# The first experts on tokens sorted by group into tiles of 128, with the token tiles stationary and the weights moving

## The chip, the cores and the metric

The kernel is one program on one core of a Trainium2 chip. It holds its state in on-chip memory and streams every large weight from HBM once. The metric is the device time of one execution in microseconds (us), lower being better. PE is the matmul engine, DVE the vector engine, ACT the scalar engine, POOL the third elementwise engine, SP the engine that issues the weight transfers.

## The reference

Two blocks run one after the other, all in float32. The first has 256 tokens (272 with the meta tokens) of width 1024: a mixer, an output projection `w_out`, and then, on the normalised rows, a two-level mixture of 16 experts of hidden width 256, in 4 groups of 4:

```python
g_sel = argmax(x @ w_rg + b_rg)                    # one group of 4 for each token
p_g = softmax(group logits)[g_sel]
e_prob = softmax(expert logits of that group)      # 4 experts
top_p, top_i = top_k(e_prob, 2); top_p /= sum(top_p)
combine[token, expert] = p_g * top_p               # zero for 14 of 16 experts
for e in range(16):
    h = silu(x @ w_gate[e]) * (x @ w_up[e])        # 1024 -> 256
    y = y + combine[:, e:e+1] * (h @ w_down[e])    # 256 -> 1024
```

The second block has two layers on 512 tokens (256 of them a context): two gated feed-forward parts each, attention between them, all modulated by a vector that is itself a product with a large matrix, `w_ada`. The result must agree to float32 accuracy.

## The kernel before

**Weights in units.** Every weight is streamed as a *unit* of 1 MB (128 partitions of 2048 elements) into one of two `raw` buffers, by SP. ACT writes its high part `w_hi` (L601), DVE its low part `w_lo`, which is `raw` minus `w_hi` (L1046). The rows of the tokens are split likewise (`u_hi`, `u_lo`), and PE forms each product as three matmuls, high by high, high by low and low by high (L1864, L1865, L1866 in `products`). A 128x128 block of weights is stationary, and the tokens move, 256 columns in the first block's experts and 512 in the second block.

**The experts.** All 256 tokens go through all 16 experts. In `moe_a` (32 units, 48 matmuls of 256 columns each) PE makes gate and up; ACT takes silu, DVE multiplies by the share `comb` of the token (L1564) and by the other product (L1567), ACT makes the high part of the hidden rows and POOL the low part (`hm_lo`, L1785). In `moe_b` (16 units of 48 such matmuls) all the hidden rows are multiplied by `w_down`, which adds into the rows `h`. The routing (logits L2320 on PE, then some 40 small operations of 128x8 on DVE) stands after the first expert unit's split and runs beside the first units.

**Beside them.** Each quarter chunk of the modulation vector (1 MB of `w_ada`) is loaded by ACT and summed into `ada_acc` by four operations of 128x512 on DVE (L1067; L1064 for the first two of a chunk). PE sums each of the four chunks over partitions with 16 matmuls of one column (L2048). POOL squares the context rows for a mean (L1808 to L1811); DVE's reciprocal of it is L1603. During `moe_b` DVE and ACT also make the normalised context rows (`l0a`) of the second block. Then comes `f1a`, the second block's first feed-forward, whose unit 0 runs first on 256 rows at a time.

**Order.** Each engine runs its program in the order written, with semaphores between engines; loops `linear`, `ffn_up` and `ffn_down` go over units, and what stands beside a unit is called from them by its number. SP loads a unit when the low and high parts of the one that had its buffer are done.

## Time and profile before

| | |
|---|---|
| three runs | 2247.23, 2250.8 and 2251.64 us, median 2250.8 |
| the profiled execution | span 2245.4 us from first to last instruction; its own time beside the span is not given |
| busy share of the span | PE 97%, DVE 61%, ACT 34%, POOL 23% |
| chain that ended last | PE 85% of it, DVE 8%, ACT 3%, DMA 2% |
| first expert matmul | 150.80 us |
| end of the experts, first matmul of f1a | 443.37 us |
| first 512-column matmul of f1a unit 1 | 457.06 us |
| DMA in the whole span | 314.68 MB, mean 140 GB/s |

The profile is of one execution. A time is from the start of the span. "Busy" does not count waiting, but an instruction that is held up once started is counted as busy for as long as it takes. A duration in a group is the mean, and matmuls overlap, so their rate is read from starts that follow one another.

### The profile page before, as it was taken

The numbers are of one execution on the slowest core, as the hardware profiler recorded it, in microseconds if no ns is written. First come the engines' busy times: TensorE is split into PE (matmuls) and PEld (weight loads), VectorE is DVE, ScalarE is ACT, GpSimd is POOL, SyncE is SP. The second block draws the span as 40 slices with busy tenths as digits, with TensorE's granted clock in tenths as the row PEclk, the third lists the DMA queues.
The fourth block names the chain that finished last, engine by engine and source line by source line (L and its number), as shares of the span: only waits on it lengthen the run. The fifth ranks groups of instructions, "written<-read, shape, count | busy, mean of one in ns | idle before, by whom it ended". The sixth has DMA issues, their size and how long they took to land.

```text
span 2245.4 us, 31895 instructions
## 1 busy us (share of the span) xinstructions
PE 2185.8 (97%) x13297; PEld 1905.4 (85%) x13297; DVE 1368.7 (61%) x1770; ACT 764.9 (34%) x1075; POOL 517.5 (23%) x243
## 2 busy tenths in 40 slices
PE   7989999999999999999999999999999999899998
PEld 7889999988888888757988888898888888679998
DVE  6567875577775247796677772246655226765443
ACT  4344444432222232374322222242222223454443
POOL 0014542122221100153122221112222110243431
PEclk9999999999999999999999999999999999999999
DMA  5347876656664336301366653346663336205664
GB/s 163 106 103 213 220 224 182 176 169 175 177 173 115 92 104 180 95 20 57 110 175 185 183 155 91 97 113 187 187 187 110 96 97 168 80 1 144 179 170 147
DMA packets 474005, 314.68 MB, mean 140 GB/s; under 512 B 27503, under 2 KB 435958, under 8 KB 473862
## 3 DMA queue, kind: packets, MB, share of 16 engines
q1 hardware_dynamic: 434304, 237.02, 37.8%
q10 hardware_dynamic: 39558, 75.64, 10.8%
q8 instruction: 105, 1.72, 0.3%
q14 instruction: 38, 0.31, 0.0%
HBM read 311.56 MB, written 1.05 MB: 139 GB/s over the span
## 4 chain that ended last, share of the span: by engine, by line
PE 85%; DVE 8%; ACT 3%; DMA 2%; issue 1%; SPq 1%; POOL 0%; DVEq 0%; ACTq 0%
PE ps L1864 26%; PE ps L1866 25%; PE ps L1865 25%; DVE w_lo L1046 3%; PE ps L2048 2%; ACT w_hi L601 2%; PE ps L1857 2%; PE ps L2491 1%; PE ps L2453 1%; DVE st L1703 1%; DMA raw<-in_w_ffn_down 1%; DVE u_lo L1139 1%; DMA raw<-in_w_in 1%; SPq L572 1%; DVE tmp_a L1131 1%
## 5 line engine op out<-in xcount | busy, mean ns | idle before, releaser
L1864 PE MATMUL ps<-u_hi,w_hi 128*128 128x256 f32 (+2 forms) x2624 | 887.3, 338 | 16.5 <-DVE u_lo L1139 6.2
L1866 PE MATMUL ps<-u_hi,w_lo 128*128 128x256 f32 (+2 forms) x2624 | 875.6, 334 | 0.0
L1865 PE MATMUL ps<-u_lo,w_hi 128*128 128x256 f32 (+2 forms) x2624 | 875.2, 334 | 0.0
L1046 DVE TENSOR_TENSOR w_lo<-raw,w_hi 128x2048 fp32r<-128x2048 f32 (+1 forms) x238 | 504.4, 2119 | 341.2 <-ACT w_hi L601 340.9
L601 ACT CAST w_hi<-raw 128x2048 fp32r<-128x2048 f32 (+1 forms) x238 | 418.4, 1758 | 468.7 <-PE ps L1866 411.9
L1864 PEld LDWEIGHTS ps<-u_hi,w_hi 128*128 128x128 f32 x2624 | 500.4, 191 | 69.8 <-DVE w_lo L1046 9.7
L1866 PEld LDWEIGHTS ps<-u_hi,w_lo 128*128 128x128 f32 x2624 | 500.2, 191 | 49.0
L1865 PEld LDWEIGHTS ps<-u_lo,w_hi 128*128 128x128 f32 x2624 | 500.7, 191 | 46.9
L1785 POOL TENSOR_TENSOR hf_lo<-tmp_b,hf_hi 128x512 fp32r<-128x512 f32 (+1 forms) x88 | 240.6, 2734 | 713.2 <-ACT hf_hi L744 713.2
L1067 DVE SCALAR_TENSOR_TENSOR ada_acc<-ada_w,sc_c,ada_acc 128x512 f32<-128x512 f32 x448 | 348.3, 834 | 7.8 <-DMA ada_w<-in_w_ada 2.0
L1864 PE MATMUL ps<-hf_hi,w_hi 128*128 128x512 f32 (+1 forms) x770 | 270.6, 351 | 1.0 <-DVE w_lo L1046 0.8
L1865 PE MATMUL ps<-hf_lo,w_hi 128*128 128x512 f32 (+1 forms) x770 | 269.3, 350 | 0.0
L1866 PE MATMUL ps<-hf_hi,w_lo 128*128 128x512 f32 (+1 forms) x770 | 269.3, 350 | 0.0
L741 ACT ACTIVATE tmp_a<-ps 128x512 f32<-128x512 f32 (+1 forms) x88 | 47.9, 545 | 614.1 <-PE ps L1866 449.7
L1198 DVE TENSOR_TENSOR tmp_b<-tmp_a,ps 128x512 f32<-128x512 f32 (+1 forms) x88 | 54.6, 621 | 185.5 <-ACT tmp_a L741 185.5
L1864 PEld LDWEIGHTS ps<-hf_hi,w_hi 128*128 128x128 f32 x770 | 144.9, 188 | 22.4 <-DVE w_lo L1046 1.0
L1866 PEld LDWEIGHTS ps<-hf_hi,w_lo 128*128 128x128 f32 x770 | 144.9, 188 | 21.1
L1865 PEld LDWEIGHTS ps<-hf_lo,w_hi 128*128 128x128 f32 x770 | 144.8, 188 | 21.1
L1800 POOL TENSOR_TENSOR sq_sum<-sq_sum,tmp_b 128x512 f32<-128x512 f32 (+1 forms) x37 | 75.4, 2038 | 297.8 <-ACT tmp_b L627 250.4
L1845 POOL TENSOR_SCALAR s<-s,st 128x512 f32<-128x512 f32 (+1 forms) x48 | 78.9, 1648 | 143.7 <-DVE st L1718 143.7
L1785 POOL TENSOR_TENSOR hm_lo<-tmp_b,hm_hi 128x256 fp32r<-128x256 f32 x32 | 75.3, 2353 | 123.5 <-ACT hm_hi L864 123.5
L1256 DVE SCALAR_TENSOR_TENSOR h<-ps,gate,h 128x256 f32<-128x256 f32 x50 | 22.3, 480 | 105.7 <-PE ps L1866 105.7
(314 smaller groups left out, 1903.9 us busy)
## 6 DMA issues: line engine op xcount, KB each, us to landing
ada_w<-in_w_ada ACTq DMA_DIRECT2D x144, 512.0 KB, 4.0
raw<-in_w_ffn_gate SPq DMA_DIRECT2D x88, 512.0 KB, 4.0
raw<-in_w_ffn_up SPq DMA_DIRECT2D x88, 512.0 KB, 5.3
raw<-in_w_in SPq DMA_DIRECT2D x52, 512.0 KB, 5.0
...
```

Of the source, the lines that this page charges most:

```text
L601: nc.scalar.copy(w_hi[:, slot, 0:elems], raw[:, slot, 0:elems]).then_inc(hi_done.sem, 1)
L741: nc.scalar.activation(tmp_a[:, n % 2, 0:T], ps[:, 2 * (g % 2), 0:T], ACT.Silu).then_inc(sig["silu"].sem, 1)
L1046: tt(w_lo[:, slot, 0:elems], raw[:, slot, 0:elems], w_hi[:, slot, 0:elems].bitcast(F32), ALU.subtract).then_inc(lo_done.sem, 1)
L1067: ins = stt(out=ada_acc[:, v, :], in0=ada_w[:, slot, kk, :], scalar=sc_c[:, k, v:v + 1], in1=ada_acc[:, v, :], op0=ALU.mult, op1=ALU.add)
L1198: tt(tmp_b[:, n % 2, 0:T], tmp_a[:, n % 2, 0:T], ps[:, 2 * (g % 2) + 1, 0:T], ALU.mult).then_inc(acc_free.sem, 1)
L1785: tt(lo[:, n, 0:T], tmp_b[:, n % 2, 0:T], hi[:, n, 0:T].bitcast(F32), ALU.subtract).then_inc(sig["lo"].sem, 1)
L1800: tt(sq_sum[:, 0:T], sq_sum[:, 0:T], tmp_b[:, k % 2, 0:T], ALU.add).then_inc(n["summed"].sem, 1)
L1845: ins = nc.gpsimd.tensor_scalar(s[:, x, 1, c0:c1], s[:, x, 1, c0:c1], st[:, i % 4, 0, nq + q:nq + q + 1], None, ALU.mult)
L1857: return nc.tensor.transpose(dst, src, ident[0:n, 0:n])
L1864: mm(acc, w1, m_hi, start=(first and i == 0), stop=False)
L1865: mm(acc, w1, m_lo, start=False, stop=False)
L1866: ins = mm(acc, w2, m_hi, start=False, stop=(last and i == n - 1))
```

## The change

The numbers of lines in this section are those of the changed kernel.

**Sorting.** After the group of each token is known, DVE works out a slot for it (position within its group, by three matmuls against a triangle; a token past the 128th of its group goes to a fifth tile) and builds a 0/1 matrix `place` (two tiles of 128 tokens by 640 slots). PE turns the rows `u_hi` and `u_lo` to tokens by columns (`turn_tokens`, 32 transposes), and `gather` multiplies them by `place` into the tiles: four tiles, one for each group, and a spill tile for the group that has more than 128 tokens. ACT and DVE copy them out as `x_hi` and `x_lo`. The shares of the slots come by 20 small float32 matmuls (`slot_shares`).

**Twenty steps.** A step is one tile through one expert: five tiles of four experts. `up_part` has the tile stationary and the weights moving, 8 blocks by 3 matmuls of 512 columns (256 of gate, 256 of up). ACT takes silu, DVE multiplies by share and up in one operation (`hid`, L1756, 128x256), PE turns `hid` by two transposes during the next step, ACT and DVE split it (`ht_hi`, `ht_lo` L1724), and `down_part` adds 12 matmuls of 512 columns to two banks that hold the tile's output for its four experts. Each four steps, ACT and DVE split a tile's output (`tile_rest`); at the end `scatter` multiplies the tiles by `place` turned, 80 matmuls of 256 columns, back into rows that are added to `h`.

**Units.** There are 60 units of expert weights instead of 48, three for a step, since the spill tile's group is loaded again, its number read by SP from a register. They go through a ring of five raw buffers (two old, three in space not yet used) and three for the parts.

**Low parts.** `vector_cols` divides them: POOL makes the whole low part of the second unit (`M0 + 1`, 128x2048), and half (128x1024) of the unit of `w_down` of each step; DVE makes the rest. In all POOL makes 11 of 60 units' worth. The low part of the hidden rows, which POOL made, is DVE's now.

**Moved.** The context rows' squares go from beside the experts to the time right after the context rows come out of PE (about 52 us), ahead of the mixer's masks on POOL. Their root and reciprocal go from `moe_b` to ahead of the routing. The mean squares of the final norm are made by token, by PE from squares of ACT. The normalised context rows come in the last two steps. A quarter of the modulation vector stands in each of the steps 1 to 16. The load of the last unit of `w_out` comes after a wait for the mixer's sums, behind a table of 400 KB, the router's weights and unit `M0 + 1`.

```diff
+        M0, M1 = st_moe["u0"], st_moe["u0"] + st_moe["units"]
+
+        def gate_unit(i):
+
+            return M0 + max(3 * i - 1, 0)
+
+        def down_unit(i):
+
+            return M0 + min(3 * i + 4, 3 * STEPS - 1)
+
+        downs = {down_unit(i): i for i in range(STEPS)}
+        RAW_RING, W_RING = (2, 3, 4, 0, 1), (0, 1, 2)
+        raw_of = [RAW_RING[(u - M0) % 5] if M0 <= u < M1 else u % 2 for u in range(N_UNITS)]
+        w_of = [W_RING[(u - M0) % 3] if M0 <= u < M1 else u % 2 for u in range(N_UNITS)]
...
+        def vector_cols(u):
+
+            if u >= N_UNITS:
+                return 0
+            return 0 if u == M0 + 1 else 4 if u in downs else KD
...
+            nc.vector.reciprocal(rstd[:, SEQ:T2], rstd[:, SEQ:T2]).then_inc(ev["ctx_rstd"], 1)
...
+            def tile_low(k):
+
+                dve.wait_ge(ev["gathered"], 2 * k + 2)
+                nc.vector.tensor_copy(x_lo[:, k, :], ps[:, GATHER_BANKS[k % 2][1], :]).then_inc(ev["x_low"], 1)
...
+            def hidden_low(i):
+
+                dve.wait_ge(ev["ht_high"], i + 1)
+                tt(ht_lo[:, i % 2, :, :], ps[:, 5, HID * (i % 2):HID * (i % 2) + HID].rearrange("p (k t) -> p k t", k=2),
+                   ht_hi[:, i % 2, :, :].bitcast(F32), ALU.subtract).then_inc(ev["ht_low"], 1)
...
+            for i in range(STEPS):
+                if i:
+                    hidden_low(i - 1)
+                    split_lo(gate_unit(i) + 3)
...
+                dve.wait_ge(ev["m_silu"], i + 1)
+                stt(out=hid[:, i % 2, :], in0=gated_up[:, i % 2, :], scalar=share[:, i // 4, i % 4:i % 4 + 1],
+                    in1=ps[:, i % 2, HID:2 * HID], op0=ALU.mult, op1=ALU.mult).then_inc(ev["m_hid"], 1)
+                work, complete = ada_at("moe", i)
+                if complete is not None:
+                    ada_out(complete)
+                split_lo(gate_unit(i) + (4 if i else 3))
+                split_lo(gate_unit(i) + (5 if i else 4))
...
+                for c, quarter in work:
+                    ada_quarter(c, quarter)
...
+                pool.wait_ge(hi_done.sem, u + 1)
+                n = vector_cols(u)
+                tt(w_view(w_lo, u_lo, u)[:, n:KD, :], raw_view(u)[:, n:KD, :], w_view(w_hi, u_hi, u)[:, n:KD, :].bitcast(F32),
+                   ALU.subtract).then_inc(lo_pool.sem, 1)
...
+            pool.wait_ge(rows_out.sem, rows_out.at(12))
+            context_squares()
...
             square_sums("ffn1", SEQ)
-            pool.wait_ge(rows_out.sem, rows_out.at(12))
-            ffn_up(moe_sig, SEQ, MOE_F, hm_hi, hm_lo, context_squares)
-            square_sums("end1", T2, norm_of["l0a"])
+            split_lo(M0 + 1)
+            for i in range(STEPS):
+                split_lo(down_unit(i))
...
+            def gather(k):
+
+                if k >= 2:
+                    pe.wait_ge(ev["x_high"], k - 1)
+                    pe.wait_ge(ev["x_low"], k - 1)
+                for bank, ut in zip(GATHER_BANKS[k % 2], (ut_hi, ut_lo)):
+                    for t in range(2):
+                        ins = mm(ps[:, bank, :], ut[:, t, P * k:P * k + P], place[:, t, 0:4 * P], start=(t == 0), stop=(t == 1))
+                    ins.then_inc(ev["gathered"], 1)
...
+            def up_part(i, k):
+
+                u = gate_unit(i) + k // 4
+                j = 2 * (k % 4)
+                m_hi, m_lo = [tile_out(i // 4, part)[:, k, :] for part in range(2)]
+                acc = wide(i % 2)
+                high, low = two_eighths(u, w_hi, u_hi, j), two_eighths(u, w_lo, u_lo, j)
+                mm(acc, m_hi, high, start=(k == 0), stop=False)
+                mm(acc, m_lo, high, start=False, stop=False)
+                ins = mm(acc, m_hi, low, start=False, stop=(k == KD - 1))
+                if k % 4 == 3:
+                    ins.then_inc(unit_done.sem, 1)
+
+            def turn_hidden(i):
+
+                pe.wait_ge(ev["m_hid"], i + 1)
+                if i:
+                    pe.wait_ge(ev["ht_low"], i)
+                for k in range(2):
+                    c0 = HID * (i % 2) + P * k
+                    ins = turn(ps[:, 5, c0:c0 + P], hid[:, i % 2, P * k:P * k + P], P)
+                ins.then_inc(ev["hid_turned"], 1)
+
+            def down_part(i):
+
+                u, e = down_unit(i), i % 4
+                begin(u, None)
+                pe.wait_ge(ev["ht_low"], i + 1)
+                if e == 0 and i:
+                    pe.wait_ge(ev["y_low"], i // 2)
+                if i == 0:
+                    pe.wait_ge(ev["x_low"], KD)
+                for half in range(2):
+                    acc = wide(2 + half)
+                    for k in range(2):
...
+            pe.wait_ge(ev["places"], 1)
+            gather(0)
+            gather(1)
+            begin(M0, None)
+            for k in range(KD):
+                if k == 4:
+                    begin(M0 + 1, None)
+                pe.wait_ge(ev["x_high"], k + 1)
+                pe.wait_ge(ev["x_low"], k + 1)
+                up_part(0, k)
+                if k + 2 < KD:
+                    gather(k + 2)
+            slot_shares()
+            for i in range(1, STEPS):
+                begin(gate_unit(i), None)
+                if i >= 2:
+                    pe.wait_ge(ev["m_hid"], i - 1)
+                if i == STEPS - PER_GROUP:
+                    pe.wait_ge(ev["xb_high"], 2)
+                    pe.wait_ge(ev["xb_low"], 2)
+                for k in range(4):
+                    up_part(i, k)
+                    if k == 1:
+                        turn_hidden(i - 1)
+                complete = ada_at("moe", i)[1]
+                if complete is not None:
+                    ada_sums(complete)
+                begin(gate_unit(i) + 1, None)
+                for k in range(4, KD):
+                    up_part(i, k)
+                if i in (2, 3):
+                    gather_spill(i - 2)
+                if 5 <= i < 5 + TILES:
+                    turn_places(i - 5)
+                down_part(i - 1)
+            turn_hidden(STEPS - 1)
+            pe.wait_ge(ev["place_rows"], TILES)
+            scatter(0, 0, TILES - 1)
+            scatter(1, 0, TILES - 1)
+            down_part(STEPS - 1)
```

DVE in the middle of `moe_a` before: one unit after another, `tmp_a` and `tmp_b` being silu times share and the hidden rows.

```order
L1564 TENSOR_TENSOR tmp_a<-tmp_a,comb 128x256
L1567 TENSOR_TENSOR tmp_b<-tmp_a,ps 128x256
L1046 TENSOR_TENSOR w_lo<-raw,w_hi 128x2048
L1067 SCALAR_TENSOR_TENSOR ada_acc<-ada_w,sc_c,ada_acc 128x512 x4
L1564 TENSOR_TENSOR tmp_a<-tmp_a,comb 128x256
L1567 TENSOR_TENSOR tmp_b<-tmp_a,ps 128x256
L1046 TENSOR_TENSOR w_lo<-raw,w_hi 128x2048
```

DVE in the middle of the steps now; the first row is the hidden rows of the step before, and `u_lo` is the third buffer for low parts.

```order
L1724 TENSOR_TENSOR ht_lo<-ps,ht_hi 128x256
L1181 TENSOR_TENSOR u_lo<-h,u_hi 128x8x256
L1756 SCALAR_TENSOR_TENSOR hid<-gated_up,share,ps 128x256
L1181 TENSOR_TENSOR w_lo<-raw_92,w_hi 128x2048
L1181 TENSOR_TENSOR w_lo<-raw_93,w_hi 128x1024
L1200 SCALAR_TENSOR_TENSOR ada_acc<-ada_w,sc_c,ada_acc 128x512 x4
L1724 TENSOR_TENSOR ht_lo<-ps,ht_hi 128x256
```

One step has two and a half low parts, of 5120 elements, one quarter of the vector and two operations of 256, where two units of `moe_a` had two low parts, four operations of 256 and one quarter.

PE at the start of a step now (`x_hi`, `x_lo` the tile's rows, stationary, `u_hi`, `u_lo` the first unit's parts, moving), with the turn of the hidden rows of the step before.

```order
L2590 MATMUL ps<-u_hi,x_lo 128x512
L2591 MATMUL ps<-u_lo,x_hi 128x512
L2589 MATMUL ps<-u_hi,x_hi 128x512
L2590 MATMUL ps<-u_hi,x_lo 128x512
L2591 MATMUL ps<-u_lo,x_hi 128x512
L2035 MATMUL ps<-base,hid 128x128 x2
L2589 MATMUL ps<-u_hi,x_hi 128x512
```

And at its end, where the last block of `up_part` (here from the first buffer for parts) and the end of the one before are followed by the first of `down_part`'s 12.

```order
L2591 MATMUL ps<-w_lo,x_hi 128x512
L2589 MATMUL ps<-w_hi,x_hi 128x512
L2590 MATMUL ps<-w_hi,x_lo 128x512
L2591 MATMUL ps<-w_lo,x_hi 128x512
L2620 MATMUL ps<-w_hi,ht_hi 128x512
L2621 MATMUL ps<-w_hi,ht_lo 128x512
L2622 MATMUL ps<-w_lo,ht_hi 128x512
```

The turn stands after 6 of 24 matmuls, and what it yields must be split by ACT and DVE before `down_part`, which comes 18 matmuls later.

POOL before, from the norm ahead of the router into the experts.

```order
L1800 TENSOR_TENSOR sq_sum<-sq_sum,tmp_b 128x256 x4
L1785 TENSOR_TENSOR hm_lo<-tmp_b,hm_hi 128x256 x9
L1808 TENSOR_TENSOR rstd<-h 128x256
L1785 TENSOR_TENSOR hm_lo<-tmp_b,hm_hi 128x256
L1810 TENSOR_TENSOR tmp_b<-h 128x256
```

POOL now at the same place.

```order
L1994 AFFINE_SELECT sT<-sT 64x256 x4
L1958 TENSOR_TENSOR sq_sum<-tmp_b 128x256
L1961 TENSOR_TENSOR sq_sum<-sq_sum,tmp_b 128x256 x4
L1981 TENSOR_TENSOR w_lo<-raw_92,w_hi 128x2048
L1981 TENSOR_TENSOR w_lo<-raw,w_hi 128x1024
L1981 TENSOR_TENSOR w_lo<-raw_93,w_hi 128x1024
L1981 TENSOR_TENSOR w_lo<-h,w_hi 128x1024
```

The norm's sums are followed at once by the low part of the whole unit `M0 + 1`, and then by a half for each step; between them POOL only waits.

## Rows read from the trace of the kernel before

**Rows 1.** Stretches: length, busy time of each engine, granted clock, DMA share, GB/s.
```profile
40.00:60.00 20.00, 19.63 (x154) 19.34 (x153) 16.09 (x29) 13.42 (x21) 0.00 (x0) 1.00 0.43 139
140.00:150.00 10.00, 7.14 (x37) 4.12 (x37) 6.62 (x19) 6.17 (x13) 0.21 (x1) 0.69 0.38 102
150.80:443.37 292.57, 290.46 (x2409) 287.81 (x2407) 212.75 (x256) 123.92 (x148) 104.11 (x53) 1.00 0.72 198
443.37:457.06 13.69, 13.69 (x114) 13.58 (x113) 9.51 (x20) 8.48 (x14) 0.00 (x0) 1.00 0.29 77
940.00:960.00 20.00, 15.49 (x95) 11.54 (x93) 13.55 (x29) 12.97 (x37) 5.79 (x5) 1.00 0.19 58
```

**Rows 2.** Timeline of PE: start, duration, line, operands, shape, count.
```profile
151.04 0.28 PE L1866 MATMUL ps<-u_hi,w_lo 128*128 128x256 f32 x1
151.16 0.28 PE L1864 MATMUL ps<-u_hi,w_hi 128*128 128x256 f32 x1
...
462.54 0.39 PE L1864 MATMUL ps<-u_hi,w_hi 128*128 128x512 f32 x1
462.77 0.39 PE L1865 MATMUL ps<-u_lo,w_hi 128*128 128x512 f32 x1
```

**Rows 3.** Groups by shape, 150.80 to 457.06: count, busy us, mean ns, idle before.
```profile
L1046 DVE TENSOR_TENSOR w_lo<-raw,w_hi 128x2048 fp32r<-128x2048 f32 x49 | 112.2, 2289 | 48.8 <-ACT w_hi L601 48.6
...
L1785 POOL TENSOR_TENSOR hm_lo<-tmp_b,hm_hi 128x256 fp32r<-128x256 f32 x32 | 75.3, 2353 | 123.5 <-ACT hm_hi L864 123.5
...
L1067 DVE SCALAR_TENSOR_TENSOR ada_acc<-ada_w,sc_c,ada_acc 128x512 f32<-128x512 f32 x56 | 47.6, 904 | 0.0
L1567 DVE TENSOR_TENSOR tmp_b<-tmp_a,ps 128x256 f32<-128x256 f32 x32 | 13.5, 421 | 1.4 <-ACT tmp_a L872 0.4
...
L1811 POOL TENSOR_TENSOR rstd<-rstd,tmp_b 128x256 f32<-128x256 f32 x7 | 6.3, 907 | 0.5
```

**Rows 4.** Timelines of POOL and DVE where both are at work, and where POOL is idle.
```profile
902.29 6.80 POOL L1839 TENSOR_TENSOR bias_rev<-bias_rev,att 128x3072 f32<-128x3072 f32 x1 [86.07 <-DMA bias_rev<-in_rpb_nbr]
...
902.74 6.63 DVE L1683 TENSOR_TENSOR proj<-tmp_a 128x256 f32<-128x256 f32 x1
...
1905.66 6.76 POOL L1839 TENSOR_TENSOR bias_rev<-bias_rev,att 128x3072 f32<-128x3072 f32 x1 [64.49 <-DMA bias_rev<-in_rpb_nbr]
...
1907.76 1.22 DVE L1686 COPY proj<-ps 128x1024 f32<-128x1024 f32 x1 [4.15 <-PE ps L1866]
1910.41 4.15 DVE L1046 TENSOR_TENSOR w_lo<-raw,w_hi 128x2048 fp32r<-128x2048 f32 x1 [1.43 <-ACT w_hi L601]
...
499.23 2.07 DVE L1067 SCALAR_TENSOR_TENSOR ada_acc<-ada_w,sc_c,ada_acc 128x512 f32<-128x512 f32 x3
```

**Rows 5.** Timelines of ACT and DVE in the steps before the first experts.
```profile
142.51 1.89 ACT L601 CAST w_hi<-raw 128x2048 fp32r<-128x2048 f32 x1
...
144.74 0.42 DVE L1121 TENSOR_TENSOR u_lo<-tmp_a,u_hi 128x256 fp32r<-128x256 f32 x1 [0.25 <-ACT u_hi L658]
...
150.00 2.28 DVE L1046 TENSOR_TENSOR w_lo<-raw,w_hi 128x2048 fp32r<-128x2048 f32 x1
...
156.33 0.17 DVE L1498 TENSOR_TENSOR r4c<-prob,r1a 128x8 f32<-128x8 f32 x1
156.53 0.17 DVE L1499 TENSOR_TENSOR r4c<-r4c,base 128x8 f32<-128x8 f32 x1
```

**Rows 6.** Groups by shape over the whole span, of DVE, PE and ACT.
```profile
L1603 DVE RECIPROCAL rstd<-rstd 128x256 f32<-128x256 f32 x1 | 1.7, 1742 | 0.0
...
L2048 PE MATMUL ps<-base,ada_acc 128*128 128x1 f32 x512 | 59.2, 244 | 1.0 <-DVE ada_acc L1067 1.0
...
L787 ACT COPY v_tok<-ps 64x512 f32<-64x512 f32 x4 | 2.3, 581 | 4.0 <-PE ps L1857 4.0
```

**Rows 7.** DMA of 1900 to 1912 us in 40 slices: busy tenths, and GB/s.
```profile
DMA  8563562564477899999999999999765431110000
GB/s 138 57 57 66 32 55 36 59 73 79 125 202 245 274 355 365 366 384 379 382 386 372 355 345 348 345 352 365 242 229 181 150 120 44 48 44 10 0 0 0
```

More of the change, by code:

```diff
@@ L221, in program @@
         yp_hi, yp_lo = RP["yp_hi"], RP["yp_lo"]
-        hm_hi, hm_lo, comb = R2.values()
-        _, wr, wr_hi, wr_lo, rb, lg, r4a, r4b, r4c, oh_g, r1a, r1b, r1c, pg, r16, oh1, prob, combT, lgT, comb_hi, comb_lo, pick = RR.values()
+        (x_hi, x_lo, xb_hi, xb_lo, ut_hi, ut_lo, place, ht_hi, ht_lo, gated_up, hid, raw3, raw4, lg, r4a, r4b, r4c, oh_g,
+         r1a, r1b, r1c, pg, r16, oh1, prob, at4, slot, share, over4, over, over_int) = RM.values()
+        table = RT["table"]
+        wr, wr_hi, wr_lo, rb, lgT = RR.values()
+        place_t, sq_rows = RS["place_t"], RQ["sq_rows"]
+        before_me, slot_ids = table[:, 0:P], table[:, P:P + SLOTS]
+        first_slot, spill, group_ids = [table[:, P + SLOTS + 4 * j:P + SLOTS + 4 * j + 4] for j in range(3)]
         hf_hi, hf_lo = R3.values()
@@ L547, in _ @@
+            unit(down_unit(STEPS - 1), down_before)
             for l in range(2):
@@ L2049, in ada_sums, with ffn_up @@
                 ins.then_inc(ada_sum.sem, 1)
-            def ffn_up(stg, T, n_units, ada, routing=None, opening=None, halves=2, hooks=None, whole=False):
-                for n in range(n_units):
+            def ffn_up(stg, T, n_units, ada, opening=None, halves=2, whole=False, n0=0):
+                for n in range(n0, n_units):
                     u, g = stg["u0"] + n, stg["g0"] + n
-                    if opening and halves == 2 and not hooks:
+                    if opening and halves == 2:
                         if n == 0:
@@ new lines, in turn_hidden @@
+            def turn_hidden(i):
+                pe.wait_ge(ev["m_hid"], i + 1)
+                if i:
+                    pe.wait_ge(ev["ht_low"], i)
[9 more added lines that the diff above has]
+                    pe.wait_ge(ev["y_low"], i // 2)
+                if i == 0:
+                    pe.wait_ge(ev["x_low"], KD)
+                for half in range(2):
+                    acc = wide(2 + half)
+                    for k in range(2):
+                        m_hi, m_lo = ht_hi[:, i % 2, k, :], ht_lo[:, i % 2, k, :]
+                        high, low = [two_eighths(u, w, uw, 4 * k + 2 * half) for w, uw in ((w_hi, u_hi), (w_lo, u_lo))]
+                        first, final = e == 0 and k == 0, e == 3 and k == 1
+                        mm(acc, m_hi, high, start=first, stop=False)
+                        mm(acc, m_lo, high, start=False, stop=False)
+                        ins = mm(acc, m_hi, low, start=False, stop=final)
+                ins.then_inc(unit_done.sem, 1)
```

658 lines of the change are left out of this document (408 added, 250 removed).

## The prediction

> **What bounds the kernel now.** I read the busy time by stretch first. In the experts, 150.80 to 443.37, PE is busy 290.46 of 292.57 us at a granted clock of 1.00, DVE 212.75, ACT 123.92, POOL 104.11, at 198 GB/s [rows 1]. So matmul columns set this stage; DVE has a quarter of its time left, POOL nearly two thirds. From 443.37 the last sums, the final norm and f1a's first unit take 13.69 [rows 1]. All that the change rewrites lies before 457.06, where f1a's unit 1 begins; what follows keeps its work. I therefore forecast when that point comes. The profiled execution's span is 2245.4; its own time isn't given, and the runs' median is 2250.8, 5.4 above the span, so I add the difference in us to that median.
>
> **PE's new work.** Matmuls of 256 columns start 0.12 apart (151.04, 151.16), those of 512 columns 0.23 (462.54, 462.77) [rows 2]. Before, 48 units of 48 matmuls are 2304 x 0.12 = 276. Now a step has 24 + 12 of 512 columns, 36 x 0.23 = 8.3, and two transposes (about 0.25): 8.5, or 170 for twenty. Every fourth step adds the vector's 16 sums, 0.24 each [rows 6] but overlapping, so at most 3.9; I take half of that, and it falls into PE's waits. If PE alone counted, some 106 us would go, less the sorting.
>
> **DVE's new step.** A low part of 2048 takes 2.29 us [rows 3], of which I take 2.21 where the next operation follows at once, since starts then follow a little closer than the durations; one of 1024 then 1.15. A step has 2 x 2.21 + 1.15 = 5.57 of low parts, `ht_lo` 0.36 and `hid` 0.46 (nearest row: a multiply of 256 with PSUM in it, 0.42 [rows 3]), and four of the vector's operations: three take 2.07 with POOL silent, so start to start 0.66 [rows 4], four 2.64. That is 9.0 of own work, already more than PE's 8.5.
>
> **POOL's share.** The question is what DVE does while POOL makes its half. POOL's add of 3072 elements at 902.29 takes 6.80; DVE's operation on two SBUF inputs, 256 wide, that starts at 902.74 takes 6.63, though its like takes about 0.4: it ends with POOL's. At 1910.41 a low part takes 4.15 with POOL's 6.76 from 1905.66 in its way: it begins 2.0 before POOL ends at 1912.42 and then runs its 2.2. But a copy from PSUM (1907.76) takes 1.22, started and finished beside POOL [rows 4]. And in the experts POOL's own 256-wide operation takes 2353 ns under DVE's low parts, 907 where it squares [rows 3]. So the two exclude each other wherever DVE reads two SBUF tensors, as each low part and each of the vector's operations does. POOL needs 6.80 / 3072 = 2.2 ns for an element, DVE 1.1. A half of 1024 takes POOL 2.2 to 2.3, in which DVE may do `ht_lo` and `hid`, which read PSUM, but nothing else: it saves DVE 1.1 and costs it up to 2.2. Bounds of the period of a step: below, 5.57 + 2.64 + 0.82 = 9.0 with a little for handing over, 9.4, if POOL's half always falls in DVE's waits; above, 9.0 + 2.2 = 11.2. I take **11.2**, since DVE's row has no wait of its own to put it in and 902.74 shows the whole of POOL's operation in DVE's way. PE then waits some 2.6 a step in front of `down_part`, for `ht_low` behind DVE's queue and for the half.
> The Trainium skill (Perfetto Trace Analysis, Optimizing Scalar/DVE Operations) says that GpSimd and DVE share an SBUF read port, so that moving work between them might not help. That speaks against this share, and the rows agree; by it the period is 11.2, by a half that costs DVE nothing 9.4.
>
> **Transfers.** A step loads three units of 1.05 MB and a quarter of 0.52: 3.67 MB. In 1900 to 1912, with the same packets and the engines at 9 of 10 or more, 345 to 386 GB/s moved [rows 7]: at 370 that is 9.9 us, below 11.2, with five buffers to smooth it; this stage before moved 198 GB/s [rows 1]. Transfers are the next bound if DVE's were lower.
> The Trainium skill (DMA: Bandwidth & Descriptors, Bandwidth) has 341 GB/s for 1 MB. By that a step's loads would take 10.8, still below 11.2.
>
> **Before the steps.** (1) The context squares are 15 operations on POOL, some 0.9 each [rows 3], now at about 52 to 68, where DVE is 16.09 of 20 busy [rows 1] with low parts whose unit PE waits for: below nothing (all in gaps), above 13; I take 3, as only half of DVE's work there reads two SBUF tensors and it has 4 us of slack. (2) POOL makes the low part of `M0 + 1`, 2048 x 2.2 = 4.5, as soon as its high part is there (before 142.51 + 1.89 = 144.4). That is just when DVE makes `u_lo` row by row, from 144.74 to 150.00 [rows 5], each an operation on two SBUF inputs for which the router's matmuls wait. The rows come 4.4 later; DVE's own low part at 150.00 is no longer before the routing, but didn't hold up PE. Bounds 0 and 4.5. (3) The logits ended just before the first expert matmul, which came at 150.80; they thus end at 150.8 + 3 + 4.4 = 158.2. Before, the routing ran beside the first units; now nothing can be gathered before it. Copy, addition, the reciprocal of 256 that now stands in front (1.74 [rows 6]) and some 20 small operations at 0.2 (156.33, 156.53 [rows 5]) make 6.7 to `place`. ACT meanwhile has eight copies of 512 at 0.58 [rows 6], the high part of unit 2 (1.9), exponentials and a table load (I take 1.3), so `x_hi` starts late: the first `up_part` about 11 after the logits (an estimate: 4.6 + 1.9 + 1.3 + 0.6 is 8.4, and the last copies wait for PE's turns). Then gather (4 matmuls) and up (3) alternate, 7 x 0.23 = 1.6, six times, two ups alone at 0.7: 10.9. The first step's up part ends at 158.2 + 22 = 180.
>
> **Steps and end.** From there to the end of `down_part` of step 0 I count 5.7 (half of an up part and the 12 matmuls of the down part, 2.8 + 2.8). Sixteen periods of 11.2: 179.2. Steps 17 to 19 have no quarter, but 18 and 19 have the context's rows, some 3 us of DVE each: 8.8 + 11.5 + 11.5, and 3.2 for the last turn and down part: 35. Then 80 matmuls of 256 columns by 0.12 (9.6, of which a part runs before the last down part), sums into `h`, means, root, reciprocal, spread and the rows of the norm: with 13.69 before from the same kind of chain, I take 21, and 2.7 of f1a. Sum: 180 + 5.7 + 179.2 + 35 + 23.7 = 423.6, against 457.06: 33.5 earlier.
>
> **The clock.** At 140 to 150 PE is busy 7.14 of 10 us and was granted 0.69, that is part of the time 1.2 GHz of 2.4 [rows 1]. The sorting and the end are as sparse, and some 18 us of PE's work lie there: 18 x (1/0.69 - 1) = 8 more. Sum: 25 less than before, 2250.8 - 25 = **2226**.
>
> **Rivals.**
> *A, likeliest, 0.50:* as summed, DVE and POOL in each other's way; 2210 to 2240, with (1), (2) and the period (11.0 to 12) inside.
> *B, 0.22: POOL's half is hidden.* For it: DVE waits for ACT's high parts now (48.8 us in this stage [rows 3]), and POOL would start in such a wait. Against it: those waits exist because DVE is not the bound. The period is 9.4, held up by transfers at 9.9: 16 x 1.3 = 21, and with nothing for (1) and (2) up to 7: about 2198.
> *C, 0.13: transfers bound.* 325 GB/s on average is asked for at 11.2, and no stretch of before holds more than 198 for long [rows 1]. At 300 GB/s a step takes 12.2: 16 more, 2242; above 11.2 + 25/16 = 12.8 a step (287 GB/s) it is no longer a gain.
> *D, the other side, 0.13: the clock falls inside the steps.* PE would be busy 8.5 of 11.2 in each, 76%. At 940 to 960 it was busy 77% and kept 1.00; at 140 to 150 71% and got 0.69 [rows 1]. The steps lie between. A step at 1.2 GHz takes PE 17 in place of 8.5, so its period 17. It decides from 25 us, that is in 4.3 of 19 steps at 5.8 each; in half of them it gives 2226 + 55 = 2281, in all 2336.
> The Trainium skill (Perfetto Trace Analysis, Matmul Optimizations) says that the matmul engine scales power with utilisation and that matmuls should come back to back in batches. The steps don't; by that rule D would be what happens, and the traces bear it out in one of two stretches.
> That the work isn't saved (PE's matmuls slower than 0.23 with weights moving) has nothing for it; 0.02 for this or another cause.
>
> **How the numbers follow.** 0.2% of 2250.8 is 4.5 us, about what a measurement can tell from no change. A, B and nearly all of C are faster; a tail of C and of A is within 0.2%; D is slower: faster 0.83, same 0.04, slower 0.13. The range leaves out D and the lower end of B: 2190 to 2256.
>
> **What the profile would show.** The period, read from `hid` to `hid`: 11.2 with DVE busy throughout (A), 9.4 to 9.9 with DMA at 9 of 10 (B), above 12 with ACT waiting for DMA (C). POOL's halves: 2.2 each, with a DVE low part or operation of the vector stretched beside them. PE's wait in front of `down_part`, on DVE. The granted clock in the steps: 1.00, else D. Unit `M0 + 1` on POOL from 147 to 152 with `u_lo` behind it; the first `up_part` near 169, the first step's end near 180, f1a's unit 1 near 424 to 432. Wrong I would be above all if the period is not DVE's, or if the sorting takes PE much longer than 22.

## The result, and the profile after

The changed kernel takes 2279.6 us (median of four runs, 2278.6 to 2283.0) against 2251.0 in four runs of the kernel before: 1.0134 times the time, 95% interval 1.0121 to 1.0146. It is 28.6 us slower, where 25 less were forecast. The profiled execution took 2278.6, its span is 2276.9, 31.5 more than before.

The page of the changed kernel, part 1:

```profile
PE 2148.1 (94%) x11957; PEld 1821.0 (80%) x11957; DVE 1395.0 (61%) x1776; ACT 792.5 (35%) x1088; POOL 507.4 (22%) x233
```

PE is busy 38 us less than before (2185.8 on that page), and its share fell from 97% to 94%: work went, and waits came. The stretches, with the same columns as [rows 1]: the mixer's start; the router; from the first expert matmul to the last one's start; the first of the four long steps; and from there to f1a's unit 1.

```profile
40.00:60.00 20.00, 17.74 (x142) 17.53 (x141) 16.36 (x28) 12.67 (x19) 7.19 (x7) 1.00 0.44 140
155.00:165.00 10.00, 7.94 (x46) 4.68 (x46) 8.50 (x18) 4.86 (x11) 1.11 (x1) 0.68 0.30 105
173.81:462.82 289.01, 226.71 (x926) 180.98 (x926) 222.46 (x224) 139.50 (x132) 68.61 (x20) 0.87 0.72 237
231.66:251.23 19.57, 14.51 (x55) 11.93 (x54) 11.19 (x13) 5.37 (x7) 3.40 (x1) 0.70 0.73 250
462.82:487.82 25.00, 24.71 (x200) 24.11 (x199) 11.86 (x28) 12.58 (x29) 5.14 (x7) 1.00 0.01 2
```

The experts took 292.57 us before; they take 289.01 now and begin 23 later, with PE busy 226.71 in place of 290.46. So 64 us of PE's work are gone from the stretch, and hardly any of its length. That long step has PE at a granted clock of 0.70 and DVE busy for 11.2 of its 19.6 us. Some starts on PE (columns as in [rows 2]): the first expert matmul, the last matmul of the first step's up part, a wait in the steps with what follows it, and f1a's first matmul of 512 columns, which came at 457.06 before and was forecast near 424 to 432.

```profile
173.81 0.77 PE L2589 MATMUL ps<-w_hi,x_hi 128*128 128x512 f32 x1 [0.15 <-issue]
...
185.71 0.40 PE L2591 MATMUL ps<-w_lo,x_hi 128*128 128x512 f32 x1
...
242.32 3.57 PE L2226 MATMUL ps<-base,ada_acc 128*128 128x1 f32 x16 [5.06 <-DVE ada_acc L1200]
245.75 0.77 PE L2589 MATMUL ps<-w_hi,x_hi 128*128 128x512 f32 x1
246.33 0.63 PE L2590 MATMUL ps<-w_hi,x_lo 128*128 128x512 f32 x1
...
487.82 0.40 PE L2042 MATMUL ps<-u_hi,w_hi 128*128 128x512 f32 x1
```

The steps are read from the operation `hid` on DVE. In between stand the last quarter of a chunk of the modulation vector and the low part of the hidden rows.

```profile
188.49 0.48 DVE L1756 SCALAR_TENSOR_TENSOR hid<-gated_up,share,ps 128x256 f32<-128x256 f32 x1
...
197.15 0.47 DVE L1756 SCALAR_TENSOR_TENSOR hid<-gated_up,share,ps 128x256 f32<-128x256 f32 x1
...
231.66 0.47 DVE L1756 SCALAR_TENSOR_TENSOR hid<-gated_up,share,ps 128x256 f32<-128x256 f32 x1
...
238.62 3.64 DVE L1200 SCALAR_TENSOR_TENSOR ada_acc<-ada_w,sc_c,ada_acc 128x512 f32<-128x512 f32 x4
242.19 0.41 DVE L1724 TENSOR_TENSOR ht_lo<-ps,ht_hi 128x256 fp32r<-128x256 f32 x1
...
251.23 0.48 DVE L1756 SCALAR_TENSOR_TENSOR hid<-gated_up,share,ps 128x256 f32<-128x256 f32 x1 [6.43 <-ACT gated_up L1001]
...
263.79 0.47 DVE L1756 SCALAR_TENSOR_TENSOR hid<-gated_up,share,ps 128x256 f32<-128x256 f32 x1
```

From 231.66 to 251.23 are 19.6 us, from 251.23 to 263.79 are 12.6. Over all steps the distances are 8.7, 11.3, 11.6, 11.6, **19.6**, 12.6, 11.6, 13.1, **19.9**, 12.7, 11.6, 12.9, **18.2**, 12.3, 11.6, 13.1, **18.5**, 10.4, 12.4. The forecast period of 11.2 is there in the plain steps (11.3 to 11.6); each fourth step takes 7 to 8 more. Who waited for whom in the steps (sum, times, longest):

```profile
PE ps L2620 <- DVE ht_lo L1724: 30.1, 13, 3.8
DVE hid L1756 <- ACT gated_up L1001: 25.6, 4, 6.9
DVE w_lo L1181 <- ACT w_hi L720: 22.8, 23, 2.0
...
PE ps L2226 <- DVE ada_acc L1200: 19.7, 4, 5.1
```

PE waits for `ht_lo` in front of `down_part`, where it was forecast, but 30.1 us in 13 waits and not 2.6 in each step. But four times it waits 5 us for `ada_acc`. In step 5, 9, 13 and 17 it has to sum a finished chunk between the two halves of `up_part`, and that chunk's last quarter is the last thing in DVE's queue for the step before (238.62 to 242.26). In the kernel before PE was behind DVE, and its sums waited 1.0 us in all [rows 6]; now DVE is the later one. DVE, for its part, finds nothing to do until that `up_part` is through, 6.4 us at 251.23: the wait isn't a shift between the two, but lost by both. Behind it PE runs its matmuls of 512 columns 0.43 apart (245.75 to 246.33 is the first, 0.58), that is at 1.2 GHz, until 249.7.

The steps before the last three long ones take 12.9 to 13.1. There the chain goes the other way round, from PE over ACT to DVE (here from 275.4 to 288.5).

```profile
275.12 0.63 PE L2622 MATMUL ps<-w_lo,ht_hi 128*128 128x512 f32 x1
275.55 0.63 PE L2620 MATMUL ps<-w_hi,ht_hi 128*128 128x512 f32 x1
...
278.04 1.91 ACT L720 CAST w_hi<-h 128x2048 fp32r<-128x2048 f32 x1 [5.20 <-PE ps L2622]
...
279.99 1.23 DVE L1181 TENSOR_TENSOR w_lo<-h,w_hi 128x1024 fp32r<-128x1024 f32 x1 [1.96 <-ACT w_hi L720]
```

PE's down part runs at 1.2 GHz here (0.43 apart), ACT waits for its end before it can write the next high part, and DVE waits 1.96 for ACT, where it waits 0.41 in a step of 11.6.

At the end there is another wait, on ACT, DVE and PE.

```profile
450.47 1.90 ACT L720 CAST w_hi<-raw 128x2048 fp32r<-128x2048 f32 x1 [5.91 <-DMA raw<-in_w_ffn_up]
455.12 0.91 ACT L849 ACTIVATE u_hi<-tmp_a,mod 128x256 fp32r<-128x256 f32 x2 [2.75 <-DVE tmp_a L1264]
...
457.79 0.35 ACT L984 CAST ht_hi<-ps 128x256 fp32r<-128x256 f32 x1
...
458.32 0.42 DVE L1724 TENSOR_TENSOR ht_lo<-ps,ht_hi 128x256 fp32r<-128x256 f32 x1
...
458.88 0.77 PE L2620 MATMUL ps<-u_hi,ht_hi 128*128 128x512 f32 x1 [12.27 <-DVE ht_lo L1724]
```

PE turns the hidden rows of the last step at 444.0, but in ACT's order their split stands behind that of f1a's second unit, which waits 5.9 for its load, and behind the last four context rows, which wait for DVE. PE stands still for 12.3 us with one `down_part` and most of the scattering to do.

Ahead of the steps: on DVE a unit's low part in the output projection, first in the kernel before, then in the changed one; behind it a row of `u_lo`; then POOL.

```profile
125.89 2.29 DVE L1046 TENSOR_TENSOR w_lo<-raw,w_hi 128x2048 fp32r<-128x2048 f32 x1 [1.31 <-ACT w_hi L601]
```

```profile
132.91 2.29 DVE L1181 TENSOR_TENSOR w_lo<-raw,w_hi 128x2048 fp32r<-128x2048 f32 x1 [1.30 <-ACT w_hi L720]
...
152.24 4.15 DVE L1254 TENSOR_TENSOR u_lo<-tmp_a,u_hi 128x256 fp32r<-128x256 f32 x1 [0.62 <-ACT u_hi L777]
```

```profile
151.61 4.50 POOL L1981 TENSOR_TENSOR w_lo<-raw,w_hi 128x2048 fp32r<-128x2048 f32 x1 [4.45 <-ACT w_hi L720]
```

DVE's work at 133 is 7.0 later, and the row that meets POOL's 4.50 takes 4.15 in place of 0.42.

### The profile page after: what moved, and what is told of

Read it like the earlier page. It is cut to its first block, busy times and chain, and to the rows that moved or that the text cites. A ratio compares the mean times of both kernels' runs of the same rounds, so it can differ in the third digit from the quotient of the medians.

```text
span 2276.9 us, 29268 instructions
## 1 busy us (share of the span) xinstructions
PE 2148.1 (94%) x11957; PEld 1821.0 (80%) x11957; DVE 1395.0 (61%) x1776; ACT 792.5 (35%) x1088; POOL 507.4 (22%) x233
## 3 DMA queue, kind: packets, MB, share of 16 engines
q10 hardware_dynamic: 39558, 75.64, 10.4%
## 4 chain that ended last, share of the span: by engine, by line
PE 81%; DVE 11%; ACT 4%; DMA 2%; issue 2%; SPq 0%; POOL 0%; DVEq 0%; ACTq 0%
PE ps L2042 22%; PE ps L2044 22%; PE ps L2043 22%; ACT w_hi L720 3%; DVE ada_acc L1200 3%; PE ps L2226 3%; DVE w_lo L1181 2%; PE ps L2035 2%; PE ps L2825 1%; PE ps L2787 1%; PE ps L2620 1%; PE ps L2622 1%; PE ps L2621 1%; DVE st L1864 1%; DVE tmp_a L1264 1%
## 5 line engine op out<-in xcount | busy, mean ns | idle before, releaser
L2042 PE MATMUL ps<-u_hi,w_hi 128*128 128x512 f32 (+2 forms) x2112 | 742.9, 352 | 17.3 <-DVE u_lo L1272 7.0
L2044 PE MATMUL ps<-u_hi,w_lo 128*128 128x512 f32 (+2 forms) x2112 | 731.6, 346 | 0.0
L2043 PE MATMUL ps<-u_lo,w_hi 128*128 128x512 f32 (+2 forms) x2112 | 731.3, 346 | 0.0
L1181 DVE TENSOR_TENSOR w_lo<-raw,w_hi 128x2048 fp32r<-128x2048 f32 (+1 forms) x221 | 451.1, 2042 | 310.1 <-ACT w_hi L720 310.1
L720 ACT CAST w_hi<-raw 128x2048 fp32r<-128x2048 f32 (+1 forms) x222 | 387.8, 1748 | 486.9 <-PE ps L2044 404.6
L2042 PEld LDWEIGHTS ps<-u_hi,w_hi 128*128 128x128 f32 x2112 | 403.2, 191 | 70.1 <-DVE w_lo L1181 9.3
L2044 PEld LDWEIGHTS ps<-u_hi,w_lo 128*128 128x128 f32 x2112 | 402.8, 191 | 48.9
L2043 PEld LDWEIGHTS ps<-u_lo,w_hi 128*128 128x128 f32 x2112 | 403.3, 191 | 46.9
L1961 POOL TENSOR_TENSOR sq_sum<-sq_sum,tmp_b 128x512 f32<-128x512 f32 (+1 forms) x32 | 62.3, 1947 | 250.6 <-ACT tmp_b L744 249.8
L1981 POOL TENSOR_TENSOR w_lo<-raw,w_hi 128x1024 fp32r<-128x1024 f32 (+1 forms) x16 | 55.9, 3494 | 178.4 <-ACT w_hi L720 178.4
```

The lines of the kernel that those rows point to most:

```text
L720: nc.scalar.copy(w_view(w_hi, u_hi, u), raw_view(u)).then_inc(hi_done.sem, 1)
L1181: tt(low, full, high.bitcast(F32), ALU.subtract).then_inc(lo_done.sem, 1)
L1961: tt(sq_sum[:, 0:T], sq_sum[:, 0:T], tmp_b[:, k % 2, 0:T], ALU.add).then_inc(n["summed"].sem, 1)
L1981: tt(w_view(w_lo, u_lo, u)[:, n:KD, :], raw_view(u)[:, n:KD, :], w_view(w_hi, u_hi, u)[:, n:KD, :].bitcast(F32), ALU.subtract).then_inc(lo ...
L2042: mm(acc, w1, m_hi, start=(first and i == 0), stop=False)
L2043: mm(acc, w1, m_lo, start=False, stop=False)
```

## The experiments

All kernels were run beside the kernel before, which had 2248.6, 2247.9 and 2248.7 in the three sets; the numbers below are medians, against 2279.6 for the changed kernel. Beside that one the kernel before had 2251.0, so a difference across sets is sure to some 3 us only; for the small ones the distances in the traces are given as well.

**e1_sums_later: the vector's sums later.** PE sums a chunk behind the step's down part; DVE takes it over one step later.

```diff
-                complete = ada_at("moe", i)[1]
-                if complete is not None:
-                    ada_sums(complete)
                 begin(gate_unit(i) + 1, None)
...
                 down_part(i - 1)
+                complete = ada_at("moe", i)[1]
+                if complete is not None:
+                    ada_sums(complete)
```

> Against the changed kernel's 2279.6. Theory Q (queue order): in steps 5, 9, 13 and 17 PE waits about 5 us for the last quarter of the modulation vector, which DVE does at the very end of the step before, and then works at half clock for some 4 us; those four steps take 18.2 to 19.9 us where the others take 11.6 to 13.1. With the sums behind the step's down part the four waits go and nothing new waits but the next quarter's first operation on DVE, by 1 us: 4 x 6.5 = 26 less, 2254, granted clock 1.00 in these steps. Rival R (DVE is the bound anyway): DVE's work is as long as before, PE waits for the hidden rows' low part instead, and only the slower sums are saved: 4 x 2 = 8 less, 2272.

2257.7, 22 less: theory Q, a little under its 26. The four long distances are now 13.1, 13.1, 13.0 and 13.1; the others are within 0.3 but for two (12.3 became 11.2, and 10.4 became 12.4). The granted clock did not come back to 1.00, which the theory had expected: the stretch of 200 to 300 has 0.92 (0.89 before the edit).

```profile
200.00:300.00 100.00, 85.22 (x367) 67.95 (x367) 90.12 (x82) 55.04 (x51) 27.64 (x8) 0.92 0.92 307
```

**e2_last_turn_first: the last hidden rows first.**

```diff
                 split_hi(gate_unit(i) + (4 if i else 3))
+                if i == STEPS - 1:
+                    hidden_high(STEPS - 1)
                 if i:
                     split_hi(gate_unit(i) + 5)
...
-            hidden_high(STEPS - 1)
             tile_high(TILES - 1)
```

(and the same for `hidden_low` on DVE.)

> Only ACT's and DVE's order in the last step changes: the split of the last hidden rows comes before the split of f1a's second unit and the last four context rows. Theory Q: PE's wait of 12.3 us ahead of the last down part goes, with the slow matmuls behind it: 12 less, 2267. Rival: the second unit's split and the context rows are then late for f1a, and half of it comes back at the start of f1a: 6 less, 2273.

2276.6, 3 less, which the sets alone could differ by; it is below both theories. By the traces the way from the last `hid` to f1a's unit 1 went from 45.7 to 41.7 us, 4 less. PE's last down part does start 7.7 us earlier (451.18 for 458.88), but neither theory had seen what waits next:

```profile
463.42 0.58 PE L2633 MATMUL ps<-place_t,xb_hi 128*128 128x256 f32 x1 [7.29 <-DVE xb_lo L1732]
```

The tile's own split (`xb_lo`) still stands behind the same two items, so PE waits 7.3 there. The wait was moved, not removed.

**e3_no_pool: no low parts on POOL.** `vector_cols` gives everything to DVE; the second unit's low part stands among the copies of the gathered rows.

```diff
-            return 0 if u == M0 + 1 else 4 if u in downs else KD
+            return KD
```

> All low parts on DVE, the second unit's between two copies of the gathered rows; POOL does nothing in the steps. Theory P (the prediction's price, the half blocks DVE for all its 2.2 us and saves it 1.1): 19 x 1.1 = 21 less in the steps and 4 less ahead of the router's matmuls: 2255. Theory H (from the trace of the changed kernel, where four operations of the vector take 3.64 beside POOL against 2.64 alone): a half costs DVE 1.0 and saves 1.15, so the steps stay as they are and only the 4 us ahead of the router go: 2276. Rival W (POOL's work is free): 19 x 1.15 more in the steps, 4 less ahead: 2297.

2252.9, 26.7 less: theory P, the prediction's own price; H and W are out. DVE does some 1.1 more in each step, and the plain steps fall from 11.6 to 10.5. The rows of the changed kernel show how a half can cost twice what it saves, first POOL, then DVE:

```profile
266.91 3.46 POOL L1981 TENSOR_TENSOR w_lo<-raw,w_hi 128x1024 fp32r<-128x1024 f32 x1 [7.59 <-ACT w_hi L720]
```

```profile
268.01 4.89 DVE L1200 SCALAR_TENSOR_TENSOR ada_acc<-ada_w,sc_c,ada_acc 128x512 f32<-128x512 f32 x4
272.82 0.41 DVE L1724 TENSOR_TENSOR ht_lo<-ps,ht_hi 128x256 fp32r<-128x256 f32 x1
```

Four operations of the vector take 4.89 beside POOL's half. With POOL silent three take 2.07 [rows 4] and four 2.73 (f2_all), so 2.2 of the 4.89 are POOL's. It isn't always so much: where a tile's split, which reads PSUM, comes first, the four take 3.64 (238.62 above).

**e4_squares_late: the squares behind the masks.**

```diff
-            context_squares()
             for n in range(1, 5):
                 pool.wait_ge(ev["scores_out"], n)
...
+            context_squares()
             square_sums("ffn1", SEQ)
```

> The context rows' squares on POOL stand after its five masks (about 112 us) instead of ahead of them (52 to 69). Theory S (they cost the mixer's first part 7 us, the distance by which everything at 133 is later than before, since DVE's work there has no slack): about 7 less where they meet idle time of DVE, 2273. Rival: they cost the same where they come to stand, 2280.

2274.1, 5.5 less: theory S, if a little less than its 7. The first `hid` comes at 183.45 for 188.49, and the distances of the steps stay. The other traces say the same: the norm's first matmul of 256 columns ahead of the router starts at 146.7 to 149.6 in the six kernels here with the squares early and at 139.8 to 142.4 in the six with them late, 6.7 apart in the mean.

**f1_no_pool_sums_later: two causes together.** The edits of the first and third run.

> All low parts on DVE (2252.9 by itself) and the vector's sums behind the step's down part (22 less by itself). Theory A (two separate causes): they add up, 2231, and every step with a quarter takes 10.5 to 11.5, the four with sums no more than 12. Rival T (transfers: at 10.5 a step 350 GB/s are asked for, and the DMA engines show a share of 1.00; the four long steps were what let the buffers fill again): the others become longer, 11.5 and more with ACT waiting for DMA, and at most 10 are gained, 2243.

2230.6: they add up (2252.9 - 22 = 2231). From the second distance to the seventeenth they are 10.2 to 11.7. Transfers don't take over.

**f2_all: all of them, and the end put right.** As the run before, with the squares behind the masks, and the last tile's split, too, ahead of the second unit of f1a:

```diff
-            hidden_high(STEPS - 1)
             tile_high(TILES - 1)
+            split_hi(M1 + 1)
...
             for k in range(KD):
                 dve.wait_ge(ev["row_sums"], k + 1)
                 tt(h1[:, k, N_META:T1], row_sum(k), h1[:, k, N_META:T1], ALU.add).then_inc(acc_free.sem, 1)
+            split_lo(M1 + 1)
```

> As the run before, and the context's squares behind the masks (5.5 by itself), and at the end the last tile's split, too, ahead of f1a's second unit, whose low part now comes behind the additions into h. The end's order by itself brought 3, since PE then waited 7.3 for the tile's split instead. Theory Q: with both out of the way 10 are gained at the end, 5 at the squares: 2231 - 15 = 2216, which is faster than the kernel before. Rival: f1a's second unit is late now, and the end gives 3 as before: 2223.

2213.6, 0.985 times the kernel before (0.984 to 0.987): 34 us faster than before, 66 faster than the change as it was made. Of the 17 gained on the run before this one, 5.5 are the squares' by their own run, and the rest, some 11, is the end's: by the traces the way from the last `hid` to f1a's unit 1 went from 43.3 to 31.8 us. f1a's first matmul of 512 columns:

```profile
423.76 0.40 PE L2046 MATMUL ps<-u_hi,w_hi 128*128 128x512 f32 x1
```

**f3_all_pool_halves: POOL's halves again, in that order.**

> As the run before, but POOL makes its half of each step's down unit again (the second unit stays with DVE). Theory P: each step is 1.1 longer for DVE, 19 x 1.1 = 21 more, 2237. Rival H: in this order the halves lie in DVE's waits, 2216 or a little less.

2232.4, 18.8 more: theory P again (21), now without the waits for the sums and at the end. From the second on, the distances are 11.2 to 13.1. In 200 to 390 the vector's operations and the halves on DVE, first without POOL, then with:

```profile
L1202 DVE SCALAR_TENSOR_TENSOR ada_acc<-ada_w,sc_c,ada_acc 128x512 f32<-128x512 f32 x54 | 37.0, 744 | 0.0
...
L1199 DVE TENSOR_SCALAR ada_acc<-ada_w,sc_c 128x512 f32<-128x512 f32 x6 | 2.6, 480 | 0.0
```

```profile
L1202 DVE SCALAR_TENSOR_TENSOR ada_acc<-ada_w,sc_c,ada_acc 128x512 f32<-128x512 f32 x54 | 56.9, 1109 | 0.0
...
L1183 DVE TENSOR_TENSOR w_lo<-raw,w_hi 128x1024 fp32r<-128x1024 f32 x12 | 14.7, 1226 | 15.4 <-ACT w_hi L720 15.4
L1199 DVE TENSOR_SCALAR ada_acc<-ada_w,sc_c 128x512 f32<-128x512 f32 x6 | 9.1, 1552 | 0.0
```

54 operations go from 37.0 to 56.9 us, and the six that open a chunk from 2.6 to 9.1: 26.4 more for the 15 halves of the stretch (12 in these rows, 3 from another buffer), 1.8 for each. A half on DVE takes 1226 ns where the whole took 2288, 1.06 less. That leaves 0.7 for each half; the other 0.3 of the measured 1.0 are in DVE's waits for ACT, which grew from 1.0 to 1.3 a step.

**f4_all_half_vector: less work on DVE.** The additions of the first four chunks take half of the columns, which leaves the vector incomplete.

```diff
-                            ins = stt(out=ada_acc[:, v, :], in0=ada_w[:, slot, kk, :], scalar=sc_c[:, k, v:v + 1],
-                                      in1=ada_acc[:, v, :], op0=ALU.mult, op1=ALU.add)
+                            w = 256 if isinstance(j, int) and j < 4 else ADA_COLS
+                            ins = stt(out=ada_acc[:, v, 0:w], in0=ada_w[:, slot, kk, 0:w], scalar=sc_c[:, k, v:v + 1],
+                                      in1=ada_acc[:, v, 0:w], op0=ALU.mult, op1=ALU.add)
```

> As f2_all, but for the first four chunks of the modulation vector the additions on DVE take only half of the columns, so the vector is incomplete; the loads are whole. Theory D (DVE's own work of 10.5 bounds the step): 1.3 less in each of 16 steps, 21 less, 2195, periods of 9.2. Rival T (transfers, 3.67 MB a step at 350 to 370 GB/s, bound at 10 to 10.5): at most 8 less, 2208, with waits of ACT for DMA.

2194.7, 18.9 less, with distances of 9.4 to 10.7 from the fourth to the eighteenth: theory D. The stretch of 200 to 300 in f2_all and here (the last three numbers are the granted clock, the DMA share and GB/s):

```profile
200.00:300.00 100.00, 87.65 (x398) 70.11 (x397) 92.20 (x88) 60.60 (x56) 0.00 (x0) 0.97 1.00 336
```

```profile
200.00:300.00 100.00, 93.95 (x439) 75.10 (x438) 92.83 (x99) 66.97 (x61) 0.00 (x0) 1.00 1.08 366
```

The same loads come at 366 GB/s in place of 336. At 10.5 a step DMA is not the bound, though its share reads 1.00.

**g1_filler_at_sums and g2_all_filler_in_steps: filling PE's waits.** Twenty unused matmuls ahead of the sums in the changed kernel:

```diff
                 if complete is not None:
+                    pe.wait_ge(ev["xb_high"], 2)
+                    begin(gate_unit(i) + 1, None)
+                    for _ in range(20):
+                        mm(wide(6), tile_out(i // 4, 0)[:, 0, :], two_eighths(gate_unit(i) + 1, w_hi, u_hi, 0), start=True, stop=True)
                     ada_sums(complete)
```

> The changed kernel (2279.6) with 20 matmuls of 512 columns, 4.6 us at full clock, whose result nothing uses, in each of PE's four waits ahead of the vector's sums. It splits what such a wait costs. Theory K (wait and clock): the wait of 5.1 stays, but PE is not at 1.2 GHz behind it, so the 16 sums take 1.7 in place of 3.6 and the next ten matmuls 0.23 in place of 0.43: 4 x 3.5 = 14 less, 2266. Rival (the wait is all that counts, since DVE is behind anyway): 2280.

2271.6, 8 less: theory K, at somewhat over half its size. (Against the kernel before of its own set it is 5.7 less than the changed kernel; the traces decide for 8.) The long distances are 16.0, 17.4, 17.4 and 17.3, together 8.1 less than before. The stretch of 235 to 255 in the changed kernel and here, and the 16 sums here, which took 3.57 there:

```profile
235.00:255.00 20.00, 14.94 (x59) 12.25 (x58) 11.05 (x12) 7.58 (x8) 3.40 (x1) 0.74 0.59 203
```

```profile
235.00:255.00 20.00, 19.57 (x96) 15.80 (x95) 13.51 (x15) 10.41 (x11) 5.31 (x2) 1.00 0.68 231
```

```profile
243.20 1.95 PE L2226 MATMUL ps<-base,ada_acc 128*128 128x1 f32 x16 [0.43 <-DVE ada_acc L1200]
```

So of the 22 us that the four waits cost, some 8 are the clock behind them and, by difference, 14 the waits themselves.

> f2_all (2213.6) with six unused matmuls of 512 columns (1.4 us) ahead of the down part in steps 4 to 19, where PE waits 1.5 to 2.8 for DVE. Theory D (DVE bounds the steps, and the granted clock of 0.97 in 200 to 300 costs nothing): 2214, within 5. Rival K (the clock lengthens the steps of 11.7 against those of 10.5): eight steps by up to 1.0 less, 2206. Rival F (PE has no such room in half of the steps): 8 x 1.4 more, 2225.

Six such matmuls ahead of each down part of f2_all from step 4 on: 2214.2, the same within the spread of either (2210.2 to 2216.2): theory D. The granted clock in 200 to 390 went from 0.96 to 1.00. A pair of steps that took 11.7 and 10.9 takes 10.2 and 12.3, the same sum. So the lower clock there costs f2_all nothing.

**g3_all_reciprocal_later: the reciprocal later.** f2_all with the context's reciprocal ahead of `tile_low(7)`.

> f2_all (2213.6) with the context's reciprocal (1.75 on DVE) out of the chain from the logits to the slots, among the copies of the gathered rows, where DVE waits 4.6 in all. Theory: 1.7 less, 2212; rival: the gathering then waits for DVE's copy, no change.

2214.7, no change. From the first of the router's matmuls to the first `hid` it does take 1.4 less (147.75 to 180.09, for 147.95 to 181.74 in f2_all), but the second `hid` comes only at

```profile
180.09 0.48 DVE L1762 SCALAR_TENSOR_TENSOR hid<-gated_up,share,ps 128x256 f32<-128x256 f32 x1
...
186.57 2.29 DVE L1183 TENSOR_TENSOR u_lo<-h,u_hi 128x2048 fp32r<-128x2048 f32 x1 [1.25 <-ACT u_hi L720]
188.78 0.47 DVE L1762 SCALAR_TENSOR_TENSOR hid<-gated_up,share,ps 128x256 f32<-128x256 f32 x1
```

8.7 later where it was 7.3: the 1.4 are given back at once, though not in the rival's way, since the first `up_part` does come 1.7 earlier. DVE waits 1.25 for ACT, ACT 1.66 for PE's half of the up part, and PE runs that half at 1.2 GHz here, its matmuls 0.43 apart from 180.64 to 183.63, where f2_all has them 0.23 apart. First this run, then f2_all:

```profile
181.07 0.63 PE L2594 MATMUL ps<-u_hi,x_lo 128*128 128x512 f32 x1
```

```profile
182.36 0.40 PE L2594 MATMUL ps<-u_hi,x_lo 128*128 128x512 f32 x1
```

## Why the prediction was wrong

**What held.** The mutual exclusion of POOL and DVE, read from [rows 4], and its price of 1.1 a step: e3_no_pool's distances are 20 us shorter and f3_all_pool_halves takes 19 us longer, for nineteen steps. That rules out rival B. The period of 11.2: 11.3 to 11.6 in plain steps. DVE as the bound of the steps, shown by f4_all_half_vector and, from the other side, by the filler that changes nothing in f2_all. Transfers below their bound: rival C is out, since f4_all_half_vector moves 366 GB/s over 100 us at some 10 us a step. (Its argument that no stretch before holds more than 198 was a misreading: the page of the kernel before has 213 to 224 in three slices of 56 us.) The matmuls at 0.23. The whole sum, without the 8 for the clock, was 423.6 for f1a's unit 1, and f2_all has 423.76, with 11.1 from `hid` to `hid` in the mean; but that kernel has no halves on POOL and another order at the end, so the agreement is luck: errors that cancel.

**The step that failed: "Sixteen periods of 11.2".** It costed the queue of DVE alone and took the vector's sums as filling "PE's waits". It didn't ask what the sums wait for. A finished chunk is DVE's last item of a step, and PE asks for it between the halves of the next `up_part`, at a time when DVE is behind. The four places cost 76.2 us in place of 44.8, 31 more; with the sums later they take 52.3, and 22 of the 31 came back in the time of the kernel. The prediction named DVE's queue for PE's wait at `ht_low` and missed that the same queue has a second customer.

**The second: "3.2 for the last turn and down part".** By the rows it was 12.3 of waiting. The program's order puts the last hidden rows behind a unit whose load comes late. It cost some 11 (e2_last_turn_first gave 3 to 4, f2_all 11 with the tile's split moved as well).

**Ahead of the steps** the forecast was 6 short: the first step's up part ended at 186 (185.71 above) for 180. The squares cost 7.0 by the trace where 3 was taken, out of a range of 0 to 13 (5.5 by their run); `M0 + 1` on POOL cost 3.7 where 4.4 was taken. So the logits ended at 161.8 for 158.2. From there the first `up_part` took 12 us where 11 was taken, at a granted clock of 0.84 and 0.75 (160 to 170 and 170 to 180), and the eight blocks 12.1 for 10.9.

**Steps in general** were 12.2 in the mean of the twelve others of the sixteen, not 11.2: 12 us in all. A step behind a long one takes 12.3 to 12.7, where DVE waits 1.2 for ACT and POOL's half holds up the two operations that open a chunk (3.04 for 0.88 in f2_all). The three steps ahead of a long one take 12.9 to 13.1, by the chain from PE's slow down part shown above; DVE's wait there is 1.3 to 1.6 longer than in a plain step. The two operations of 0.6 for a tile's output, which the sum left out, fall into the long steps, where DVE waits anyway.

**The sum of it.** The first step and the end, from 186 to 462.8 without the sixteen periods, took 14 more than was taken for them, 12 of them PE's wait. 6 + 31 + 12 + 14, and 1 for the way to f1a's unit 1, make 64; measured are 487.8 - 423.6 = 64. The prediction's 8 for the clock stood on top of 423.6, and these distances contain what the clock cost: less the 8 the miss is 56, and the measured time is 54 over the forecast.

**Rival D** ended on the right side for another reason. The clock did fall (0.70 in a long step, 0.87 over the experts), but g1_filler_at_sums puts its share behind the long waits at 8 us, and g2_all_filler_in_steps finds none in the steps of f2_all. There a wait made the low clock; the low clock didn't make the wait. Two places are left: the first step, where g3_all_reciprocal_later shows 1.4 us going to it, and the three steps of 12.9 to 13.1 in the changed kernel, where the trace puts up to 1.5 us each on the slow down part. No run tested those three alone. All this is far from the 55 to 110 us of rival D. The rule of the Trainium skill (Perfetto Trace Analysis, Matmul Optimizations) that matmuls should come back to back is borne out behind waits of 5 us, where PE ran at 1.2 GHz for some 7 us, and is worth 8 of the 22 us that four such waits cost. That moving work between GpSimd and DVE might not help, as the Trainium skill says (Perfetto Trace Analysis, Optimizing Scalar/DVE Operations), is borne out: all halves back on DVE took 26.7 us off the changed kernel, with the second unit's low part.
